# Encoder block on 8 cores: the meta keys' V products split into two 64-row halves and moved beside the K products

## The chip, the cores and the metric

One Trainium2 chip, 8 cores, one launch of one program. Each core works on its own part of the batch (one whole prompt sequence of 2048 tokens and one half of a sample sequence of 8192) and no core waits for another. The metric is the device time of the slowest core in microseconds (us), the median of several runs. Engines are named as the profile names them: PE (TensorE; PEld is its weight load), DVE (VectorE), ACT (ScalarE), POOL (GpSimd) and SP (SyncE, here only a DMA queue).

## The reference

One layer, run on both request groups with shared weights: RMSNorm, one input projection, a pooling mixer and a neighbourhood attention side by side, gates, an output projection with a residual, and a last RMSNorm. The change is in the attention alone:

```
# q, k, v: (B, L, H, 64), L = 16 meta tokens + T; real tokens form a (ROWS, 64) grid
def row_block(r):
    rs = clip(r - 4, 0, rows - 8)                 # 8 grid rows of keys
    s_grid = einsum('bqhd,bkqjhd->bhqkj', q_r, k_r) * scale + bias     # 8 x 16 keys each
    s_meta = einsum('bqhd,bmhd->bhqm', q_r, km) * scale + mbias        # 16 meta keys
    p = softmax(concatenate([s_meta, s_grid], -1))
    return einsum('bhqm,bmhd->bqhd', p[..., :16], vm) + einsum('bhqkj,bkqjhd->bqhd', p_grid, v_r)
```

So every query takes part in 128 grid keys and 16 meta keys. The output of a query is the sum of a V product over the grid keys and one over the meta keys, divided by the sum of all the exponentials.

## The kernel before, in words

The program has three stages. Stage one normalises the tokens, makes K and V and stores them. Stage two makes Q and the pooled projection z and does the attention. Stage three does the gates and the output projection. All instructions are recorded in program order, each goes into the queue of its engine, and every engine works its queue off in that order. A helper (`Sched`) derives the waits from the names each operation reads and writes: a read waits for the last write of the same name in the recorded order.

In stage two the queries are cut into 14 tiles of query rows (`TILES`, counted from 0). Tiles 0 and 4 use one chunk of keys ("one-chunk tiles"), the other twelve use two. In tiles 0, 4, 5 and 13 a unit has 64 queries, in the others 128. A tile has 8 units: 4 column groups `s` by 2 head groups `G` of 8 heads. There are 112 units, numbered `ui`. The keys of a unit come in blocks of 128 (`unit_blocks`): 2 blocks in a one-chunk tile; in a two-chunk tile 3 for `s` 0 and 3 and 4 for `s` 1 and 2. The third block of `s` 0 and 3 takes 64 keys of each of two chunks ("the combined block"); in the unit with `G` = 1 it is put first. A block of a unit is a step, and there are 368 steps.

A step `(ui, b)` does the following. `p2_qk` forms the K products of 8 heads on PE: two heads at a time, one on array rows 0 to 63 and one on 64 to 127, because a head is 64 long (the trace writes 64*128; those of a combined block have 64 output rows and are written 64*64). ACT takes the exponential of the 8 heads out of two PSUM banks into `PT[ui % 2]`, slice `b`, and DVE multiplies it in place by the exponentials of the bias (`FT`, `CT` or `XT`). Then come "fills": matmuls of 128x512 of the Q and z projections (L904, L927), some 3 to 9 a step, until the tile's list is used up. Last come V products of the unit before: `p2_pv` multiplies a block's `PT` slice with V, one head at a time (65 columns; column 65 gives the sum of the exponentials), and adds them up in banks 4 and 5.

The steps are recorded in groups of two: K products of both steps, then fills and V products of the first, then of the second. So within a group of steps `(ui, 2)` and `(ui + 1, 0)` the K products, exponentials and multiplies of both stand ahead of all V products of the group.

The meta keys' exponentials of a tile lie in `PM`, 16 keys of 8 heads on 128 partitions (32 to a pair of heads). `VMb` holds the meta keys' V on the same partitions, zero outside a head's own 65 columns, so that one matmul over 128 rows and 260 columns gives the meta part of four heads. `p2_pvmeta` is that matmul. It opens each bank's sum. Bank 4 takes the four even heads (`par` = 0), bank 5 the four odd ones. `p2_norm` takes the reciprocal of the sums out of a bank (L1052) and multiplies (L1054) into `ATT`.

`pv_steps` says which V products of unit `ui - 1` go into step 0, 1 and 2 of unit `ui`: in step 0 the meta product of bank 4 and all blocks but the last, in step 1 the last block, the norm of bank 4, the meta product of bank 5 and two blocks, in step 2 the rest and the norm of bank 5. In a unit of two blocks everything of step 2 goes into step 1.

The finished `ATT` is stored from the queue of SP, in tiles 9 to 12 from the queue of POOL.

## Time and profile before

| | us |
|---|---|
| median of 3 runs | 1763.38 (1757.53 to 1893.18) |
| the profiled execution, device time | 1761.12 |
| its span on the slowest core, first to last instruction | 1759.6 |
| spans of all cores | 1748.7 to 1759.6 |
| PE busy | 1690.0 (96%) |
| stage two, 438 to 1058 us of the span: PE busy | 590.5 of 620.0 |

The profiled execution is 1.5 us longer than its span, for what lies ahead of the first and behind the last instruction, and 2.3 us under the median. The granted TensorE clock is 0.986 of full over the whole span of this core. In the rows "busy" is the time in which at least one instruction of a group ran. A matmul's own length (some 190 to 380 ns) is longer than the distance to the next one that starts behind it, because they run in a pipeline: what a matmul costs PE is read from one start to the next.

### The profile page before, as it was taken

How to read it: one execution, taken by the hardware profiler on the slowest of the kernel's cores; microseconds unless marked ns; L12 is line 12 of the kernel's file. 1: busy time of each engine (PE TensorE's matmuls, PEld its weight loads, DVE VectorE, ACT ScalarE, POOL GpSimd, SP SyncE). 2: the span in 40 equal slices, each digit the busy share in tenths (PEclk: the TensorE clock that was granted, in tenths of full speed). 3: DMA queues.
4: the chain of work that ended last, by engine and by line, in shares of the span. 5: the costliest groups of instructions: out<-in, count | busy, mean ns of one | idle time of the engine just before them, and what ended most of it. 6: DMA issues, size and time to landing. Idle time of an engine off the chain costs nothing.

```text
span 1759.6 us, 39346 instructions; the slowest of 8 cores (1748.7 to 1759.6 us)
## 1 busy us (share of the span) xinstructions
PE 1690.0 (96%) x13906; PEld 873.7 (50%) x13906; DVE 1000.9 (57%) x1907; ACT 821.3 (47%) x1219; POOL 124.3 (7%) x202
## 2 busy tenths in 40 slices
PE   7799999999999899999999998999999999999998
PEld 3344544444455555655666554444444444444443
DVE  3354544442466665766777755556655566556654
ACT  3256666331256765777777762332333233323332
POOL 1011021111100000000000020000000000000000
PEclk9899999999999999999999999999999999999999
DMA  9689778663555566666543479733454346524521
GB/s 264 218 239 282 226 240 238 200 169 136 172 141 157 149 166 176 154 179 176 146 123 98 132 214 266 187 114 109 126 174 148 86 128 162 168 88 129 139 96 61
DMA packets 163814, 289.21 MB, mean 164 GB/s; under 512 B 70627, under 2 KB 92643, under 8 KB 155047
## 3 DMA queue, kind: packets, MB, share of 16 engines
q1 hardware_dynamic: 110167, 155.04, 31.2%
q0 software_dynamic: 37184, 95.66, 19.1%
q10 hardware_dynamic: 16272, 35.99, 6.6%
q8 instruction: 116, 1.90, 0.5%
q14 instruction: 75, 0.61, 0.1%
HBM read 194.90 MB, written 100.90 MB: 168 GB/s over the span
## 4 chain that ended last, share of the span: by engine, by line
PE 79%; issue 5%; ACT 5%; DVE 4%; DMA 4%; SPq 2%; ACTq 1%; DVEq 0%; POOL 0%; POOLq 0%
PE bankpair L433 19%; PE bankpair L927 9%; PE bankpair L588 9%; PE bankpair L620 9%; PE bankpair L407 9%; PE bankpair L380 9%; PE bankpair L904 5%; PE bankpair L1039 3%; PE bankpair L1008 3%; ACT sb_PT L1014 2%; DMA sb_XSG<-xt 2%; DVE sb_PT L1020 1%; PE bankpair L567 1%; PE bankpair L368 1%; DVE sb_QT L217 1%
## 5 line engine op out<-in xcount | busy, mean ns | idle before, releaser
L1014 ACT ACTIVATE sb_PT<-bankpair 128x1024 bf16<-128x1024 f32 (+1 forms) x368 | 318.8, 921 | 152.8 <-PE bankpair L1008 112.1
L433 PE MATMUL bankpair<-sb_Wo,sb_MIX 128*128 128x512 bf16 x1536 | 336.9, 381 | 3.7 <-DVE sb_MIX L417 3.7
L433 PEld LDWEIGHTS bankpair<-sb_Wo,sb_MIX 128*128 128x128 bf16 x1536 | 150.8, 98 | 187.8 <-issue 9.1
L1020 DVE TENSOR_TENSOR sb_PT<-sb_PT,sb_FT 128x1024 bf16<-128x1024 bf16 (+1 forms) x264 | 174.8, 666 | 106.1 <-ACT sb_PT L1014 103.3
L927 PE MATMUL bankpair<-sb_Wz,sb_HT 128*128 128x512 bf16 x768 | 199.6, 388 | 3.0 <-ACT sb_PM L957 2.7
L588 PE MATMUL bankpair<-sb_HT,sb_Wk 128*128 128x512 bf16 (+1 forms) x832 | 189.7, 383 | 9.5 <-ACT sb_Wk L219 5.0
L904 PE MATMUL bankpair<-sb_HT,sb_Wq 128*128 128x512 bf16 x768 | 194.7, 382 | 1.7 <-DVE sb_QT L217 1.7
L620 PE MATMUL bankpair<-sb_Wv,sb_HT 128*128 128x512 bf16 x816 | 184.0, 379 | 0.0
L380 PE MATMUL bankpair<-sb_HT,sb_Wg 128*128 128x512 bf16 x768 | 182.6, 381 | 0.0
L441 ACT ACTIVATE sb_junk<-sb_Y 128x1024 bf16<-128x1024 f32 x48 | 50.7, 1057 | 266.3 <-DVE sb_Y L436 266.3
L407 PE MATMUL bankpair<-sb_HT,sb_Wg 128*128 128x512 bf16 x768 | 167.7, 379 | 0.0
L1039 PEld LDWEIGHTS bankpair<-sb_VP,sb_PT 128*128 128x128 bf16 x2496 | 122.2, 98 | 51.1 <-issue 4.1
L1039 PE MATMUL bankpair<-sb_VP,sb_PT 128*128 128x65 bf16 x2496 | 135.6, 194 | 3.1 <-issue 3.1
L588 PEld LDWEIGHTS bankpair<-sb_HT,sb_Wk 128*128 128x128 bf16 x832 | 80.9, 100 | 100.2 <-issue 18.6
L436 DVE TENSOR_TENSOR sb_Y<-bankpair,sb_XR 128x512 f32<-128x512 f32 x96 | 66.1, 689 | 112.2 <-PE bankpair L433 112.2
L620 PEld LDWEIGHTS bankpair<-sb_Wv,sb_HT 128*128 128x128 bf16 x816 | 79.7, 98 | 95.0
L1008 PE MATMUL bankpair<-sb_QT,sb_KR 64*128 64x128 bf16 (+3 forms) x3328 | 111.8, 213 | 13.8 <-ACT sb_PT L1014 13.5
L407 PEld LDWEIGHTS bankpair<-sb_HT,sb_Wg 128*128 128x128 bf16 x768 | 74.3, 98 | 87.8
L411 ACT ACTIVATE sb_TH<-bankpair 128x512 f32<-128x512 f32 x96 | 57.3, 597 | 114.5 <-PE bankpair L407 92.7
L1054 DVE TENSOR_TENSOR sb_ATT<-bankpair,sb_rec 128x256 bf16<-128x256 f32 (+1 forms) x224 | 94.7, 423 | 27.8 <-DVE sb_rec L1052 10.3
L380 PEld LDWEIGHTS bankpair<-sb_HT,sb_Wg 128*128 128x128 bf16 x768 | 69.6, 98 | 71.4 <-issue 1.5
L386 ACT ACTIVATE sb_TH<-bankpair 128x512 f32<-128x512 f32 x96 | 56.1, 596 | 100.9 <-PE bankpair L380 69.4
(104 smaller groups left out, 1736.3 us busy)
## 6 DMA issues: line engine op xcount, KB each, us to landing
sb_X<-xall SPq DMA_DIRECT2D x51, 512.0 KB, 5.7
sb_XR<-xall SPq DMA_DIRECT2D x48, 512.0 KB, 3.6
y<-sb_O POOLq DMA_DIRECT2D x48, 512.0 KB, 3.2
sb_HT<-hT_s SPq DMA_DIRECT2D x23, 1024.0 KB, 6.1
sb_KR<-kT_s SPq DMA_DIRECT2D x14, 1024.0 KB, 7.2
sb_UW<-u_s SPq DMA_DIRECT2D x54, 256.0 KB, 7.8
kT_s<-sb_KTs POOLq DMA_DIRECT2D x13, 1024.0 KB, 5.1
v_s<-sb_Vs POOLq DMA_DIRECT2D x49, 260.0 KB, 3.5
```

Of the source, the lines that this page charges most:

```text
L380: S.op('tensor', lambda e, pg=pg, dc=dc, kc=kc, cs=cs, N=N: e.matmul(banks[pg][:, 0:N], Wg[dc // 2][:, kc, dc % 2 * 128:dc % 2 * 128 + 128 ...
L407: S.op('tensor', lambda e, pg=pg, fc=fc, kc=kc, cs=cs, N=N: e.matmul(banks[pg][:, 0:N], Wg[4 + fc // 2][:, kc, fc % 2 * 128:fc % 2 * 128 + ...
L433: S.op('tensor', lambda e, po=po, kc=kc, cg=cg, j=j: e.matmul(banks[po][:, :], MIX[:, kc, j * 128:(j + 1) * 128], Wo[kc // 4][:, kc % 4, c ...
L588: S.op('tensor', lambda e, pb=pb, fc=fc, kc=kc, hs=hs, N=N: e.matmul(banks[pb][:, 0:N], Wk[:, kc, fc * 128:(fc + 1) * 128], HT[hs][:, kc, ...
L620: S.op('tensor', lambda e, pb=pb, cg=cg, kc=kc, hs=hs, j=j: e.matmul(banks[pb][:, :], HT[hs][:, kc, j * 128:(j + 1) * 128], Wv[:, kc, cg * ...
L904: S.op('tensor', lambda e: e.matmul(banks[pb][:, :], Wq[:, kc, fc * 128:(fc + 1) * 128], HT2[ci % 2][:, kc, :], start=(kc == 0), stop=(kc ...
L927: S.op('tensor', lambda e: e.matmul(banks[pb][:, :], src[:, kc, p * 128:(p + 1) * 128], Wz[:, kc, cg * 512:(cg + 1) * 512], start=(kc == 0 ...
L1008: S.op('tensor', lambda e, jj=jj, fc=fc, i=i, cell=cell, ncell=ncell, p0=p0, par=par: e.matmul(banks[2 * sp + par][p0:p0 + 64 * ncell, jj ...
L1014: S.op('scalar', lambda e: e.activation(out=PT[ps][0:nk, bi, :, 0:n].rearrange('p (a b) q -> p a b q', a=2), in_=bank2[sp][0:nk, :].rearra ...
L1020: S.op('vector', lambda e: e.tensor_tensor(out=PT[ps][0:nk, bi, :, 0:n], in0=PT[ps][0:nk, bi, :, 0:n], in1=bl['E'](hs), op=ALU.mult), read ...
L1039: S.op('tensor', lambda e, jj=jj, h=h: e.matmul(banks[4 + par][:, jj * 65:(jj + 1) * 65], PT[ps][0:nk, bi, par * 4 + jj, :], bl['V'][0:nk, ...
L1054: S.op('vector', lambda e: e.tensor_tensor(out=ATT[at][0:n, :].rearrange('p (a b c) -> p a b c', a=8, b=2)[:, 4 * G:4 * G + 4, par, :], in ...
```

## The change

The meta products are split by rows instead of by bank. Bank 4 now takes heads 0 to 3 of the group and bank 5 heads 4 to 7. The meta rows of heads 0 to 3 lie on partitions 0 to 63 and those of heads 4 to 7 on 64 to 127, so each bank's meta product needs 64 rows only, and the two stand together, on the two halves of the array. `VMb` shrinks from 1040 to 528 columns. The V products of the blocks are as many as before, in another order of heads, and are shared out by a new function `pv_plan`:

- unit `ui - 1`, when unit `ui` has 2 blocks (15 units, those ahead of a unit of tile 0 or 4): the meta products stand behind the K products of the group of steps 0 and 1, open both banks, and all V products and norms go into steps 0 and 1;
- when `ui` has 3 or 4 blocks and its first step is the first of a group (72 units): the meta products stand at the head of the group with step 2, ahead of its K products, and close bank 4, whose norm is recorded directly behind them. All V products of bank 5 go into step 2;
- when its first step is the second of a group (24 units): the meta products stand behind the K products of the group with step 1, and the rest is as before;
- the last unit has its V products behind the loop, as before.

In one-chunk tiles the combined block's V products now take all 128 rows; the lower 64 rows of `VC` are set to zero on DVE for that (4 times). All stores of `ATT` go through the queue of SP.

```
@@ v_combo
+                    if len(tl['ch']) == 1:
+                        S.op('vector', lambda e: e.memset(VC[w][64:128, :], 0.0), writes=[('VC', w, 1)])
@@ p2_pvmeta, p2_pv
-                def p2_pvmeta(ui, par):
-                    S.op('tensor', lambda e: e.matmul(
-                        banks[4 + par][:, 0:260], PM[t % 2][:, G, s, :], VMb[:, G, par, :, :].rearrange('p a b -> p (a b)'),
-                        start=True, stop=False), reads=[('PM', t % 2, G)] + VMR, writes=[PS(4 + par)])
+                def p2_pvmeta(ui, opens, ends=False):
+                    for half in range(2):
+                        rows = slice(64 * half, 64 * half + 64)
+                        S.op('tensor', lambda e, half=half, rows=rows: e.matmul(
+                            banks[4 + half][:, 0:260], PM[t % 2][rows, G, s, :], VMb[rows, G, 0:260],
+                            start=(opens or half == 1), stop=(ends and half == 0)), reads=[('PM', t % 2, G)] + VMR, writes=[PS(4 + half)])
-                def p2_pv(ui, par, bi, last):
+                def p2_pv(ui, half, bi, opens, last):
-                    for jj in range(4):
+                    for q in range(4):
+                        jj, par = 2 * half + q // 2, q % 2
@@ pv_steps is replaced by
+                def pv_plan(ui):
+                    nb = nblk[ui]
+                    nn = nblk[ui + 1] if ui + 1 < len(units) else 2
+                    even = ui + 1 == len(units) or first_step[ui + 1] % 2 == 0
+                    opens = even and nn == 2
+                    lead = [lambda bi=bi: p2_pv(ui, 0, bi, bi == 0 and not opens, False) for bi in range(nb - 1)]
+                    tail = lambda last: [lambda: p2_pv(ui, 0, nb - 1, False, last)]
+                    half1 = [lambda bi=bi: p2_pv(ui, 1, bi, False, bi == nb - 1) for bi in range(nb)]
+                    n0, n1 = [lambda: p2_norm(ui, 0)], [lambda: p2_norm(ui, 1)]
+                    if nn == 2:
+                        return 0 if even else 1, opens, {0: lead, 1: tail(True) + n0 + half1 + n1}
+                    if even:
+                        return 2, False, {0: lead, 1: tail(False), 2: half1 + n1}
+                    return 1, False, {0: lead, 1: tail(True) + n0 + half1[:2], 2: half1[2:] + n1}
@@ the loop over groups of two steps
                     for ui, b in steps[k:k + 2]:
                         if b == 0:
                             unit_begin(ui)
+                        if b == 2 and ui > 0 and pv_plan(ui - 1)[0] == 2:
+                            p2_pvmeta(ui - 1, False, True)
+                            p2_norm(ui - 1, 0)
+                    for ui, b in steps[k:k + 2]:
                         p2_qk(ui, b)
+                    for ui, b in steps[k:k + 2]:
+                        if b < 2 and ui > 0 and pv_plan(ui - 1)[0] == b:
+                            p2_pvmeta(ui - 1, pv_plan(ui - 1)[1])
                     for ui, b in steps[k:k + 2]:
                         unit_step(ui, b)
```

In the listings below `sb_VMb` with 128x260 is a meta product, `sb_KR` a K product, `sb_VP` or `sb_VC` with 128x65 a V product of a block, and `sb_Wz` or `sb_Wq` a fill.

On PE, in tile 0, around the K products of a group of a one-chunk tile. Before:

```order
L1039 MATMUL bankpair<-sb_VC,sb_PT 128x65 x4
L1027 MATMUL bankpair<-sb_VMb,sb_PM 128x260 [waits s_vector]
L1039 MATMUL bankpair<-sb_VP_0,sb_PT 128x65 x4
L1039 MATMUL bankpair<-sb_VC,sb_PT 128x65 x4
L1008 MATMUL bankpair<-sb_QT,sb_KR 128x64 x16
L927 MATMUL bankpair<-sb_Wz,sb_HT_0 128x512 [waits s_scalar]
L927 MATMUL bankpair<-sb_Wz,sb_HT_0 128x512 x7
L904 MATMUL bankpair<-sb_HT_1,sb_Wq 128x512 [waits d__HT2_1_False_,s_scalar]
L1027 MATMUL bankpair<-sb_VMb,sb_PM 128x260 [waits s_vector]
```

The same place after:

```order
L1042 MATMUL bankpair<-sb_VC,sb_PT 128x65 x4
L1042 MATMUL bankpair<-sb_VP_0,sb_PT 128x65 x4
L1042 MATMUL bankpair<-sb_VC,sb_PT 128x65 x4
L1011 MATMUL bankpair<-sb_QT,sb_KR 128x64 x16
L1031 MATMUL bankpair<-sb_VMb,sb_PM 128x260 [waits s_vector] x2
L930 MATMUL bankpair<-sb_Wz,sb_HT_0 128x512 [waits s_scalar]
L930 MATMUL bankpair<-sb_Wz,sb_HT_0 128x512 x7
L907 MATMUL bankpair<-sb_HT_1,sb_Wq 128x512 [waits d__HT2_1_False_,s_scalar]
```

Before, a bank's meta product stands behind fills; after, both stand directly behind the K products, and both wait for DVE, which reads the banks for the norms of the unit before.

On PE, at the entry of tile 1, the group of steps `(8, 2)` and `(9, 0)`, two combined blocks, seen from the K products on. Before:

```order
L1008 MATMUL bankpair<-sb_QT,sb_KR 64x128 [waits s_scalar]
L1008 MATMUL bankpair<-sb_QT,sb_KR 64x128 x15
L927 MATMUL bankpair<-sb_Wz,sb_HT_1 128x512 x6
L927 MATMUL bankpair<-sb_Wz,sb_HT_1 128x512 [waits s_scalar]
L927 MATMUL bankpair<-sb_Wz,sb_HT_1 128x512 x3
L1027 MATMUL bankpair<-sb_VMb,sb_PM 128x260 [waits s_vector]
L1039 MATMUL bankpair<-sb_VP_0,sb_PT 128x65 x4
```

The same place after, with the meta products ahead of it:

```order
L1042 MATMUL bankpair<-sb_VC,sb_PT 128x65 x4
L1031 MATMUL bankpair<-sb_VMb,sb_PM 128x260
L1031 MATMUL bankpair<-sb_VMb,sb_PM 128x260 [waits s_vector]
L1011 MATMUL bankpair<-sb_QT,sb_KR 64x128 [waits s_scalar]
L1011 MATMUL bankpair<-sb_QT,sb_KR 64x128 x15
L930 MATMUL bankpair<-sb_Wz,sb_HT_1 128x512 x5
L1042 MATMUL bankpair<-sb_VP_2,sb_PT 128x65 [waits s_vector]
L1042 MATMUL bankpair<-sb_VP_2,sb_PT 128x65 x3
L1042 MATMUL bankpair<-sb_VC,sb_PT 128x65 x4
L930 MATMUL bankpair<-sb_Wz,sb_HT_1 128x512
```

Between the two steps' fills there now stand V products of unit 7 (bank 5, all its blocks), and the first of them waits for DVE. They read `PT[1]`, slice 0, and the exponential and the multiply of step `(9, 0)`, recorded ahead of them in the same group, write that slice. The same happens wherever a unit of 3 blocks starts on the first step of a group: two units in each of the twelve two-chunk tiles.

## Rows read from the trace of the kernel before

**Rows 1.** The page: PE's busy time, share of the span, instructions.

```profile
PE 1690.0 (96%) x13906; PEld 873.7 (50%) x13906; DVE 1000.9 (57%) x1907; ACT 821.3 (47%) x1219; POOL 124.3 (7%) x202
```

**Rows 2.** Stage two by windows: length, busy PE, PEld, DVE, ACT, POOL, clock, DMA.

```profile
438.00:1058.00 620.00, 590.54 (x8154) 350.96 (x8152) 410.67 (x1010) 406.18 (x531) 39.94 (x50) 0.99 0.57 156
```

**Rows 3.** The group of meta products: busy us, mean ns, idle before.

```profile
L1027 PE MATMUL bankpair<-sb_VMb,sb_PM 128*128 128x260 bf16 x224 | 61.7, 275 | 7.1 <-DVE sb_rec L1052 4.4 <-DVE sb_ATT L1054 2.4
```

**Rows 4.** Timeline, tile 7, group of two combined blocks: start us, length us, engine.

```profile
754.53 0.64 PE L1008 MATMUL bankpair<-sb_QT,sb_KR 64*64 64x128 bf16 x32
755.10 1.25 PE L927 MATMUL bankpair<-sb_Wz,sb_HT 128*128 128x512 bf16 x5
756.19 0.29 PE L1039 MATMUL bankpair<-sb_VP,sb_PT 128*128 128x65 bf16 x4
756.31 1.24 PE L927 MATMUL bankpair<-sb_Wz,sb_HT 128*128 128x512 bf16 x5
...
757.15 0.69 DVE L1020 TENSOR_TENSOR sb_PT<-sb_PT,sb_CT 128x1024 bf16<-128x1024 bf16 x1 [0.22 <-ACT sb_PT L1014]
757.39 0.27 PE L1027 MATMUL bankpair<-sb_VMb,sb_PM 128*128 128x260 bf16 x1
757.50 0.41 PE L1039 MATMUL bankpair<-sb_VP,sb_PT 128*128 128x65 bf16 x8
...
757.84 0.62 PE L1008 MATMUL bankpair<-sb_QT,sb_KR 64*128 64x128 bf16 x16
```

**Rows 5.** Timeline, tile 5 (64 queries), the same kind of group.

```profile
703.18 1.04 PE L904 MATMUL bankpair<-sb_HT,sb_Wq 128*128 128x512 bf16 x4
...
703.99 0.91 DVE L1020 TENSOR_TENSOR sb_PT<-sb_PT,sb_XT 128x512 bf16<-128x512 bf16 x2
704.05 0.41 PE L1039 MATMUL bankpair<-sb_VP,sb_PT 128*128 128x65 bf16 x8
```

**Rows 6.** Timeline, tile 4 (one chunk), K products, first fill, norm of bank 5.

```profile
640.12 0.53 PE L1008 MATMUL bankpair<-sb_QT,sb_KR 64*128 64x64 bf16 x16
...
640.59 1.25 PE L904 MATMUL bankpair<-sb_HT,sb_Wq 128*128 128x512 bf16 x5
640.83 0.42 DVE L1054 TENSOR_TENSOR sb_ATT<-bankpair,sb_rec 128x256 bf16<-128x256 f32 x1
...
657.00 1.04 PE L904 MATMUL bankpair<-sb_HT,sb_Wq 128*128 128x512 bf16 x4
...
658.67 0.42 DVE L1054 TENSOR_TENSOR sb_ATT<-bankpair,sb_rec 64x256 bf16<-64x256 f32 x1
```

**Rows 7.** Timeline of PE, tile 4: V products on 64 rows; K products of whole blocks.

```profile
641.91 1.24 PE L904 MATMUL bankpair<-sb_HT,sb_Wq 128*128 128x512 bf16 x5
643.08 0.29 PE L1039 MATMUL bankpair<-sb_VC,sb_PT 64*128 64x65 bf16 x4
643.31 0.28 PE L1027 MATMUL bankpair<-sb_VMb,sb_PM 128*128 128x260 bf16 x1
...
650.61 0.41 PE L1008 MATMUL bankpair<-sb_QT,sb_KR 64*128 64x64 bf16 x16
650.95 1.04 PE L904 MATMUL bankpair<-sb_HT,sb_Wq 128*128 128x512 bf16 x4
```

**Rows 8.** What PE waited for: us in total, times, longest us.

```profile
PE bankpair L1027 <- DVE sb_rec L1052: 4.4, 5, 2.1
```

**Rows 9.** Timeline of PE: four waits, each in square brackets.

```profile
633.72 0.22 PE L1039 MATMUL bankpair<-sb_VP,sb_PT 128*128 128x65 bf16 x2 [1.39 <-issue]
...
772.68 0.40 PE L1008 MATMUL bankpair<-sb_QT,sb_KR 64*128 64x128 bf16 x8 [1.85 <-ACT sb_PT L1014]
773.60 0.54 PE L1008 MATMUL bankpair<-sb_QT,sb_KR 64*128 64x128 bf16 x8 [0.52 <-ACT sb_PT L1014]
...
1042.51 0.37 PE L1039 MATMUL bankpair<-sb_VP,sb_PT 128*128 128x65 bf16 x7 [1.68 <-issue]
```

**Rows 10.** Windows around two of them; the clock is third from the end.

```profile
773.72:777.13 3.41, 3.41 (x23) 1.56 (x20) 3.13 (x9) 1.56 (x2) 0.00 (x0) 0.50 1.02 321
...
1040.00:1045.00 5.00, 3.32 (x51) 1.91 (x48) 1.73 (x6) 2.40 (x5) 0.16 (x1) 1.00 1.03 368
```

More of the change, by code:

```diff
@@ L241, in build_program @@
         second += [('VP0_%d' % q, [128, VW], BF16) for q in range(3)] + [('VC%d' % w, [128, VW], BF16) for w in range(2)]
-        second += [('VMb', [128, 2, 2, 4, 65], BF16), ('KM', [128, KC, 32], BF16), ('HTm', [128, KC, 128], BF16)]
+        second += [('VMb', [128, 2, 264], BF16), ('KM', [128, KC, 32], BF16), ('HTm', [128, KC, 128], BF16)]
         second += [('PM%d' % i, [128, 2, 4, 128], BF16) for i in range(2)]
@@ L872, in build_program @@
                         S.op('sync', lambda e, jj=jj, par=par, p0=p0: e.dma_start(
-                            out=VMb[p0:p0 + 16, :, par, jj, :],
+                            out=VMb[p0:p0 + 16, :, (2 * (jj % 2) + par) * 65:(2 * (jj % 2) + par) * 65 + 65],
                             in_=v_d[VM + 16:VM + 32, :].rearrange('m (g q f) -> m g q f', g=2, q=8)[:, :, 2 * jj + par, :]),
@@ L985, in unit_blocks @@
                         b = dict(nk=nk, parts=[(i, 7 * w, 1, 64 * k) for k, i in enumerate(tl['ch'])], V=VC[w],
[L986 removed]
+                                 vres=[('VC', w, k) for k in range(2)])
                         if tl['xs'] is None:
@@ L1048, in p2_norm @@
                     at = (ui // 2) % 2
-                    ab = 4 + par
+                    ab = 4 + half
                     accv = lambda: banks[ab][0:n, 0:260].rearrange('p (a b) -> p a b', a=4)
-                    rs = slice(par * 4, par * 4 + 4)
+                    rs = slice(half * 4, half * 4 + 4)
+                    c0 = (8 * G + 4 * half) * 64
                     S.op('vector', lambda e: e.reciprocal(rec[0:n, rs], accv()[:, :, 64]),
-                         reads=[PS(ab)], writes=[('rec', par)])
+                         reads=[PS(ab)], writes=[('rec', half)])
@@ L1054, in p2_norm @@
                     S.op('vector', lambda e: e.tensor_tensor(
-                        out=ATT[at][0:n, :].rearrange('p (a b c) -> p a b c', a=8, b=2)[:, 4 * G:4 * G + 4, par, :], in0=accv()[:, :, 0:64],
+                        out=ATT[at][0:n, c0:c0 + 256].rearrange('p (a c) -> p a c', a=4), in0=accv()[:, :, 0:64],
                         in1=rec[0:n, rs].unsqueeze(2).to_broadcast([n, 4, 64]), op=ALU.mult),
-                         reads=[PS(ab), ('rec', par)], writes=[('ATT', at)])
-                    if G == 1 and par == 1:
+                         reads=[PS(ab), ('rec', half)], writes=[('ATT', at)])
@@ L1059, in p2_norm @@
+                    if G == 1 and half == 1:
                         t0 = tl['t0']
[L1060 removed]
+                        late.append(lambda: S.op('sync', lambda e: e.dma_start(
                             out=at_d[t0:t0 + n * 4, :].rearrange('(r c) f -> r c f', c=64)[:, 16 * s:16 * s + 16, :], in_=ATT[at][0:n, :]),
                              reads=[('ATT', at)], writes=[('at_d', t, s)], dma=('sA', at)))
[L1064 to L1076 removed]
@@ new lines, in build_program @@
+                nblk = [len(unit_blocks(u)) for u in units]
+                first_step = [sum(nblk[:i]) for i in range(len(units))]
+                def pv_plan(ui):
[12 more added lines that the diff above has]
+                    return 1, False, {0: lead, 1: tail(True) + n0 + half1[:2], 2: half1[2:] + n1}
@@ L1109, in unit_step @@
                             late.pop(0)()
-                    for f in pv_steps(ui - 1)[b] if ui > 0 and b < 3 else []:
+                    for f in pv_plan(ui - 1)[2].get(b, []) if ui > 0 else []:
                         f()
-                    if nb == 2 and b == 1 and ui > 0:
-                        for f in pv_steps(ui - 1)[2]:
-                            f()
                     if b == nb - 1:
```

31 lines of the change are left out of this document (7 added, 24 removed).

## The prediction, made before the changed kernel ran

> **What bounds the kernel now.** The page comes first: PE is busy 96% of the span, no other engine over 57% [rows 1]. All edits lie in stage two, so the windows come next: there PE is busy 590.5 of 620.0 us, DVE 411 and ACT 406 [rows 2]. PE works its queue off in order. So whatever PE saves or loses in stage two moves the end by as much, unless it falls into the 30 us in which PE waits there already. The change has to be read as PE time saved, and as PE waits removed and added. The timeline shows what things cost PE, from one start to the next: a meta product 0.11 us (757.39 to 757.50), a V product 0.03 us (four of them from 756.19 to the next fill at 756.31), a fill 0.22 us (five from 755.10 to 756.19) [rows 4].
>
> **Meta products on two halves of the array.** Before there are 224 [rows 3], 24.6 us at 0.11. After there are 112 pairs. K products already run in such pairs: the 32 quarter-array ones of [rows 4] take 0.57 us up to the first fill, 0.02 each, where 128 columns alone take more than a V product of 65 columns (0.03). So I take a pair for the price of one and save 0.11 each. In the 14 pairs that wait between their two halves (below) nothing is saved: 98 x 0.11 = **-10.8**. The bounds are -12.3 and, if the halves run one after the other, 0.
>
> **Switches of the array.** After eight V products at 0.03 (0.24) the K products start 0.34 behind the first (757.50 to 757.84), so going from whole rows to half rows costs 0.10 [rows 4]. The V products on 64 rows show both ways: they start 0.09 late behind five fills (641.91 + 1.08 = 642.99, start 643.08), and take 0.23 instead of 0.12 up to the next meta product [rows 7]. The change makes the 64-row V products of the one-chunk tiles whole. Half of them (8 places) stood between whole-row work: 8 x 0.20 = **-1.6**; the other half stood next to K products and only moves the switch. A change of the output width costs as well: the 16 K products of two whole blocks take 0.34 (650.61 to 650.95) [rows 7], the 16 of a whole and a combined block 0.47 (640.12 to 640.59) [rows 6]. A meta product is 64 rows by 128, a combined block's K product 64 by 64. They now stand side by side in 24 groups of the two-chunk tiles and 7 of the one-chunk tiles: 31 x 0.10 = **+3.1**. Elsewhere the meta pair shares the half-row stretch of its K products and adds no switch. Against this change the Trainium skill says (TensorEngine Tiling (Array Packing), "Key Properties") that changing the tiling mode drains the array, and it lists 64x128 and 64x64 as modes of their own. It gives no time. By the rule alone the moved pairs at combined blocks would pay a drain each, as I have it; the trace agrees, with 0.13 for such a change.
>
> **Waits that go.** Meta products find PE idle for 7.1 us, of which 4.4 and 2.4 end with the reciprocal and the multiply of a norm on DVE [rows 3]. The longest single wait, 2.1 [rows 8], is the last unit's, which has no cover after the change either. The other 4.7 lie where the tile's fills are used up, behind K products or between V products, and the meta products leave those places: **-4.7**, with the new waits of the one-chunk tiles counted in full below.
>
> **A new wait behind the K products in one-chunk tiles.** There both banks are opened directly behind the K products, with no fill between. Bank 5 must first be free of the norm of the unit before, which is recorded at the end of the group before. In the row that fits best the first fill starts at 640.59 and that norm's multiply ends at 640.83 + 0.42 = 641.25 [rows 6]. PE would come to the pair some 0.2 earlier than the fill did (no switch back yet, no meta product between the V products), so it waits 0.66 + 0.2 = 0.9. In the second row DVE is late (657.00 against 659.09): 2.3. The new wait itself lets DVE catch up, so I stay near the first and take 1.0. It happens in 14 units (6 in tile 0, 8 in tile 4): **+14**, bounds 9 and 20. Queued behind it on PE are the fills, and behind those the next K products. Neither ACT nor DVE profits.
>
> **A new wait in 24 groups of the two-chunk tiles.** This is the largest term. The plan for "3 or 4 blocks" puts all V products of bank 5 of unit `ui - 1` into step 2 of `ui`. When `ui` has 3 blocks, that group's second step is `(ui + 1, 0)`, and it writes the same `PT` slice 0 that the first of these V products reads. The listing shows that V product waiting for DVE behind five fills. Before, the V products of slice 0 were in step 1, a group earlier. So PE now waits for two exponentials and two multiplies of the same group. In [rows 4] the fills start at 755.10; the V products after them started at 756.19; the second multiply ends at 757.15 + 0.69 = 757.84. With 0.06 for the signal PE waits until 757.90: 1.71 us behind five fills, 1.93 behind four, 2.14 behind three. Working the list of fills out step by step gives 8 groups of 128 queries with five, 9 with four, 3 with three: 13.7 + 17.4 + 6.4 = 37.5. For 64 queries [rows 5] gives 704.90 + 0.06 against 704.05, 0.91 behind four, 0.7 behind five, 1.1 behind three: one, one and two groups, 3.8. Together **+41.3**. Nothing covers it: behind the waiting product on PE stand the other V products and five fills that are ready. The bounds are 36, if the exponentials start 0.2 earlier, and 43.
>
> That ready work doesn't pass shows in [rows 9]: at 633.72 a V product waits 1.39 us for something no engine row shows (a load of V, I suppose) with K products queued behind it. The Trainium skill has the same as a rule (TensorE: Matmul & The Clock Gate, "Step-by-step: what each phase is for"): only weight loads are pulled ahead, matmuls stay in program order. If matmuls could pass, the term would be 0.
>
> One wait is taken over: 633.72 lies behind the K products of such a group in tile 3, and the new wait of over 2 us ends later: **-1.4**.
>
> **The clock.** Behind waits of 1.85 and 0.52 us close together (772.68, 773.60) the granted clock is 0.50 for 3.41 us, the 1.2 GHz level [rows 9, 10]. Behind single waits of 1.39 and 1.68 it stays at 1.00, 2.4 GHz [rows 9, 10]. A stretch at half clock costs at most 1.7 us of matmul time; I take 1.5. The 20 new waits of 1.7 to 2.1 lie between these cases. I let five of them cost a stretch: **+7.5**, bounds 0 and 30.
>
> **At nothing.** The norms change only their columns. DVE gets four memsets of 64 rows and is busy 66% of the stage [rows 2]. `VMb` is half as long. The 16 stores that move from POOL's queue to SP's wait there for a norm, as 40 others do in tiles 0 to 8 and 13, and only loads for later tiles stand behind them; should one of these come late, it costs a wait like that at 1042.51, 1.7 us [rows 9]. Spreading the V products evenly over two groups gives PE 0.25 us more work in the lighter group of tiles 3 and 13, where PE waits for exponentials; some 1 us, not counted.
>
> **The sum.** -10.8 - 1.6 + 3.1 - 4.7 + 14 + 41.3 - 1.4 + 7.5 = +47.4. On the profiled execution's 1761.1 this gives **1808**, 2.5% over the median of 1763.4, to which the profiled execution stands 2.3 lower. A measurement of this kernel can tell about 2% from no change, that is 1799 on the slow side.
>
> **Rivals.**
> First, the clock never falls: the sum without 7.5 is 1801. For it speak the 1.39 and 1.68 that left the clock at 1.00. 25%.
> Second, the clock falls behind nearly every new wait, as behind 772.68: 20 x 1.5 in place of 7.5 gives 1831. 13%.
> Third, it does not get slower: the V products of bank 5 find slice 0 already multiplied when PE comes to them, and the 24 waits aren't there. That needs some 13 fills (2.8 us) between K products and V products, or a multiply done within 1.1 us of the K products; [rows 4] shows five fills and 2.7 us. It also holds if I misread which operation the wait is for. Then 41.3, 1.4 and 7.5 fall away and the sum is 0: 1761, and 1754 if the one-chunk waits are half as long. 8%.
> Fourth, the change does not do what it says: the two halves run one after the other and the pairs cost 0.22. Then 10.8 is lost: 1819. Against it stand the K products of [rows 4]. 4%.
> The forecast itself, 1808, has 46%; the rest, 4%, is for late loads and what I don't see.
>
> **Range and chances.** The lower bounds of the costs (36, 9, clock 0, -12.3) give +27, that is 1788; the upper ones (43, 20, clock 30) give +80, 1841. With the third rival left out, and a little of the second, 1788 to 1835 should hold 8 in 10. Slower by over 2%, above 1799: the forecast, the second and fourth rival and over half of the first, 75%. Within 2%: the third rival, the lower part of the first and of the forecast, 23%. Faster by over 2% would need 35 us saved, more than all savings together: 2%.
>
> **What the profile of the changed kernel would show.** The group of V products should have waits for DVE's multiply of `PT`, 24 of them, 40 us in all, 1.7 to 2.1 us each at 128 queries. The meta products should wait for the norm's multiply 14 times behind K products in tiles 0 and 4, some 1 us each. The pair's second half should start within 0.02 us of the first and the next matmul 0.11 to 0.2 behind it. Stage two should be 667 us long and the other two stages unchanged. The clock row should show some five more stretches at 0.50. It would be wrong if PE's waits for DVE in stage two stay under 20 us; or if the time gained between them is larger than 20 us; or if the clock falls so often that it outweighs the waits.

## The result and the profile after

The changed kernel takes 1818.7 us in the median of 4 runs (1817.0 to 1822.1), the kernel before 1763.0 beside it. The ratio is 1.033, interval 1.032 to 1.035. The forecast was 1808, the range 1788 to 1835. The profiled execution took 1817.6, its slowest core is core 3 with a span of 1816.1 us. Ratios are formed from executions alone in which no half of the chip had a lower granted clock than the other, so a median beside them can contain slower ones.

The changed kernel doesn't compute all of the attention: in 24 of the 112 units the V products of four heads take 128 keys with exponentials that belong to another unit (shown below). Its slowdown is therefore in large part the price of a fault.

The page's PE row, which answers to [rows 1]:

```profile
PE 1695.8 (93%) x13906; PEld 866.3 (48%) x13906; DVE 1008.6 (56%) x1911; ACT 821.7 (45%) x1219; POOL 114.6 (6%) x186
```

PE has nearly the same work (1690.0 before) in a longer span. POOL has 16 instructions less, the stores. Stage two by windows, which answers to [rows 2] (length, then busy PE, PEld, DVE, ACT, POOL, then clock):

```profile
438.00:1114.00 676.00, 593.87 (x8139) 342.20 (x8137) 416.85 (x1008) 406.34 (x532) 28.13 (x30) 0.98 0.52 144
```

Length minus busy PE was 29.5 us before and is 82.1 now. So nearly all of the loss is waiting. I counted stage two on every core, from its first matmul with `Wq` to the first of line 380: 617.5 us before and 676.8 now, in the mean of the eight cores. This mean is used below as the length of stage two. What lies ahead of it is unchanged (436.5 and 436.6 us). What lies behind it is 3.3 us shorter (700.2 and 696.9), of which 2.0 is less idle time of PE (4.3 and 2.3); so the whole lost a little less than stage two.

PE's waits over the whole span, the view of [rows 8] (waiting line, releaser: us in all, times, longest). L1042 is the V products, L1031 the meta products, L1011 the K products:

```profile
PE bankpair L1042 <- DVE sb_PT L1023: 39.5, 25, 2.1
PE bankpair L1011 <- ACT sb_PT L1017: 18.1, 26, 2.3
...
PE bankpair L1031 <- DVE sb_rec L1056: 10.9, 15, 2.4
...
PE bankpair L1031 <- DVE sb_ATT L1058: 5.2, 15, 0.4
PE bankpair L1042 <- DVE sb_ATT L1058: 2.8, 1, 2.8
```

The first row didn't exist before. It is the forecast's largest term, with 24 of its 25 waits. The third and fourth row are the one-chunk waits (14 units and the last one, each half once). The last row was not forecast.

**The wait for slice 0.** The timeline of a group of tile 7 in which the next unit's first block is a combined block (start us, length us, engine, line, idle before in square brackets):

```profile
787.00 0.28 PE L1031 MATMUL bankpair<-sb_VMb,sb_PM 64*128 64x260 bf16 x2
...
787.22 0.64 PE L1011 MATMUL bankpair<-sb_QT,sb_KR 64*64 64x128 bf16 x32
...
787.79 1.25 PE L930 MATMUL bankpair<-sb_Wz,sb_HT 128*128 128x512 bf16 x5
787.80 1.02 ACT L1017 ACTIVATE sb_PT<-bankpair 128x1024 bf16<-128x1024 f32 x1 [0.56 <-PE bankpair L1011]
...
788.72 1.02 ACT L1017 ACTIVATE sb_PT<-bankpair 128x1024 bf16<-128x1024 f32 x1
788.93 0.69 DVE L1023 TENSOR_TENSOR sb_PT<-sb_PT,sb_CT 128x1024 bf16<-128x1024 bf16 x1 [0.82 <-ACT sb_PT L1017]
789.84 0.69 DVE L1023 TENSOR_TENSOR sb_PT<-sb_PT,sb_CT 128x1024 bf16<-128x1024 bf16 x1 [0.22 <-ACT sb_PT L1017]
...
790.68 0.29 PE L1042 MATMUL bankpair<-sb_VC,sb_PT 128*128 128x65 bf16 x4 [1.63 <-DVE sb_PT L1023]
```

The five fills would let the V product start at 787.79 + 5 x 0.216 = 788.87. It starts at 790.68, 0.15 behind the end of the second multiply (790.53). That is 1.81 us from one start to the next, and the bracket says 1.63: the idle column counts from the modelled end of the last fill, some 0.17 later than the next matmul could have started. Worked out from the starts, the 24 waits of core 3 cost 43.2 us, and so they do on the other cores (43.1 to 43.2).

The wait is also the sign of the fault. The helper lets a read wait for the last write in recorded order, and here that write is the later unit's. So in these 24 units the products of slice 0 of four heads (bank 5) take the exponentials of unit `ui + 1` in place of their own, those of `ui - 1`, which are overwritten by then. The sums of exponentials for those heads come from the same products and are wrong with them. The wait that the helper derived keeps the read behind the write; it doesn't make it the right write.

**The one-chunk tiles.** The timeline in tile 4, with what DVE does meanwhile:

```profile
678.52 0.55 PE L1042 MATMUL bankpair<-sb_VP,sb_PT 128*128 128x65 bf16 x12
678.79 0.76 DVE L217 CAST sb_QT<-bankpair 128x256 bf16<-128x256 f32 x2 [1.81 <-PE bankpair L907]
679.00 0.41 PE L1011 MATMUL bankpair<-sb_QT,sb_KR 64*128 64x64 bf16 x16
...
679.46 0.17 DVE L1056 RECIPROCAL sb_rec<-bankpair 64x4 f32<-64x4 f32 x1
679.73 0.42 DVE L1058 TENSOR_TENSOR sb_ATT<-bankpair,sb_rec 64x256 bf16<-64x256 f32 x1
680.07 0.17 DVE L1056 RECIPROCAL sb_rec<-bankpair 64x4 f32<-64x4 f32 x1
...
680.29 0.27 PE L1031 MATMUL bankpair<-sb_VMb,sb_PM 64*128 64x260 bf16 x1 [0.88 <-DVE sb_rec L1056]
680.34 0.42 DVE L1058 TENSOR_TENSOR sb_ATT<-bankpair,sb_rec 64x256 bf16<-64x256 f32 x1
...
680.91 0.27 PE L1031 MATMUL bankpair<-sb_VMb,sb_PM 64*128 64x260 bf16 x1 [0.34 <-DVE sb_ATT L1058]
...
681.11 1.04 PE L907 MATMUL bankpair<-sb_HT,sb_Wq 128*128 128x512 bf16 x4
```

Both halves wait, one for the norm of bank 4, the other for that of bank 5, and the fills stand behind them. The second half starts 0.15 behind the end of bank 5's multiply (680.34 + 0.42 = 680.76). The first starts 0.14 behind the end of bank 4's multiply (679.73 + 0.42 = 680.15); the row names the reciprocal of bank 5 because that one ended last before it. What PE loses is set by bank 5's multiply, the last of the chain. From the last K product to the first matmul behind the pair, less the 0.26 that this takes without a wait, the 14 units lose 19.0 us in the mean of the cores. On core 3 eight of them lose 1.0 to 1.3 and six 1.5 to 2.0. In five of the six DVE is at casts of Q when the norms could begin, as at 678.79 here; in the sixth it is at a multiply of `PT`.

**The pair.** Where it doesn't wait (tile 7):

```profile
769.63 0.29 PE L1042 MATMUL bankpair<-sb_VP,sb_PT 128*128 128x65 bf16 x4
769.85 0.28 PE L1031 MATMUL bankpair<-sb_VMb,sb_PM 64*128 64x260 bf16 x2
769.97 0.61 PE L1011 MATMUL bankpair<-sb_QT,sb_KR 64*128 64x128 bf16 x16
```

Two meta products take 0.12 up to the next matmul (0.003 + 0.118), one took 0.11 before; their starts lie 3 ns apart. The four V products ahead take 0.22 instead of 0.12 [rows 4]: the switch to half rows, paid here and not behind the pair. From a pair to the K products of a combined block (787.00 to 787.22) it is 0.21 instead of 0.12: the change of shape.

**A store on SP.** The timeline of tile 12 (SPq is SP's queue):

```profile
1036.94 0.42 DVE L1058 TENSOR_TENSOR sb_ATT<-bankpair,sb_rec 128x256 bf16<-128x256 f32 x1
...
1039.26 10.76 SPq L790 DMA_DIRECT2D sb_HT<-hT_s  x4
...
1050.12 0.83 SPq L1064 DMA_DIRECT2D at_s<-sb_ATT  x1
...
1052.64 0.64 SPq L1064 DMA_DIRECT2D at_s<-sb_ATT  x1
...
1056.55 0.42 DVE L1058 TENSOR_TENSOR sb_ATT<-bankpair,sb_rec 128x256 bf16<-128x256 f32 x1 [6.39 <-DMA at_s<-sb_ATT]
...
1057.12 0.41 PE L1042 MATMUL bankpair<-sb_VP,sb_PT 128*128 128x65 bf16 x8 [2.85 <-DVE sb_ATT L1058]
```

There are two `ATT` buffers. The one that the norm at 1056.55 writes was filled by 1037.36, and its store was issued at 1050.12: four loads of `HT` stood ahead of it in SP's queue, and their issuing took 10.8 us (the store at 1052.64 is of the other buffer). DVE's norm waits until the store has landed, and PE waits for the norm. DVE waits so on all eight cores, by 3.1 to 6.7 us. PE waits behind it on six: 2.3 to 3.1 us on four, 0.4 and 0.7 on two.

### The profile page after: what moved, and what is told of

Same layout as the page of the kernel before. It is cut to its first block, busy times and chain, and to the rows that moved or that the text cites. A ratio compares the mean times of both kernels' runs of the same rounds, so it can differ in the third digit from the quotient of the medians.

```text
span 1816.1 us, 39324 instructions; the slowest of 8 cores (1805.1 to 1816.1 us)
## 1 busy us (share of the span) xinstructions
PE 1695.8 (93%) x13906; PEld 866.3 (48%) x13906; DVE 1008.6 (56%) x1911; ACT 821.7 (45%) x1219; POOL 114.6 (6%) x186
## 4 chain that ended last, share of the span: by engine, by line
PE 78%; ACT 5%; issue 5%; DMA 4%; DVE 4%; SPq 3%; ACTq 1%; DVEq 0%; POOL 0%; POOLq 0%
PE bankpair L433 18%; PE bankpair L407 8%; PE bankpair L380 8%; PE bankpair L620 8%; PE bankpair L588 8%; PE bankpair L907 7%; PE bankpair L930 7%; PE bankpair L1042 5%; PE bankpair L1011 3%; ACT sb_PT L1017 3%; SPq L479 1%; DVE sb_PT L1023 1%; DMA sb_WS<-w_in 1%; PE bankpair L368 1%; DMA at_s<-sb_ATT 1%
## 5 line engine op out<-in xcount | busy, mean ns | idle before, releaser
L907 PE MATMUL bankpair<-sb_HT,sb_Wq 128*128 128x512 bf16 x768 | 199.1, 389 | 2.6 <-DVE sb_QT L217 2.5
L930 PE MATMUL bankpair<-sb_Wz,sb_HT 128*128 128x512 bf16 x768 | 195.8, 381 | 3.0 <-ACT sb_PM L960 2.7
L1042 PE MATMUL bankpair<-sb_VP,sb_PT 128*128 128x65 bf16 x2496 | 129.4, 195 | 25.9 <-DVE sb_PT L1023 23.0
L1042 PEld LDWEIGHTS bankpair<-sb_VP,sb_PT 128*128 128x128 bf16 x2496 | 114.0, 99 | 81.2 <-issue 34.3
L1011 PE MATMUL bankpair<-sb_QT,sb_KR 64*128 64x128 bf16 (+3 forms) x3328 | 112.1, 213 | 18.6 <-ACT sb_PT L1017 18.1
L411 ACT ACTIVATE sb_TH<-bankpair 128x512 f32<-128x512 f32 x96 | 57.3, 597 | 112.2 <-PE bankpair L407 91.5
L1011 PEld LDWEIGHTS bankpair<-sb_QT,sb_KR 64*128 64x128 bf16 (+1 forms) x3328 | 82.9, 98 | 52.4 <-issue 44.9
```

The source lines that it names most:

```text
L907: S.op('tensor', lambda e: e.matmul(banks[pb][:, :], Wq[:, kc, fc * 128:(fc + 1) * 128], HT2[ci % 2][:, kc, :], start=(kc == 0), stop=(kc ...
L930: S.op('tensor', lambda e: e.matmul(banks[pb][:, :], src[:, kc, p * 128:(p + 1) * 128], Wz[:, kc, cg * 512:(cg + 1) * 512], start=(kc == 0 ...
L1011: S.op('tensor', lambda e, jj=jj, fc=fc, i=i, cell=cell, ncell=ncell, p0=p0, par=par: e.matmul(banks[2 * sp + par][p0:p0 + 64 * ncell, jj ...
L1042: S.op('tensor', lambda e, q=q, jj=jj, par=par, h=h: e.matmul(banks[4 + half][:, q * 65:(q + 1) * 65], PT[ps][:, bi, par * 4 + jj, :], bl[ ...
```

## The experiments

Line numbers move by a few between kernels: V products are L1039 (before and e7; L1041 in e6), L1042, L1043 or L1044, meta products L1027 (L1029 in e6), L1031, L1032 or L1033. Differences in us between two kernels are differences of their ratios to the kernel before, times 1761.

| kernel | ratio to before, interval | stage two, us |
|---|---|---|
| before | 1 | 617.5 |
| after | 1.0331, 1.0316 to 1.0345 | 676.8 |
| e7, before with the late slice 0 | 1.0213, 1.0188 to 1.0238 | 656.2 |
| e1, after with slice 0 in time | 1.0134, 1.0107 to 1.0161 | 639.7 |
| e2, e1 with the pair behind fills | 1.0054, 1.0040 to 1.0069 | 627.2 |
| e4, e1 with the stores on POOL | 1.0116, 1.0085 to 1.0146 | 634.1 |
| e5, e1 with another order of heads | 1.0113, 1.0094 to 1.0133 | 637.5 |
| e6, before with whole combined blocks | 1.0021, 0.9994 to 1.0048 | 613.8 |
| e9, after with full-row meta products | 1.0351, 1.0323 to 1.0379 | 678.3 |
| e3b, pair closes both banks | 1.0007, 0.9995 to 1.0019 | 619.7 |
| e10, e3b with e4 and e5 | 0.9984, 0.9957 to 1.0010 | 614.2 |

### The late slice 0 alone (e7)

```
-                        steps[1 if bi < 2 else 2].append(lambda bi=bi: p2_pv(ui, 1, bi, bi == nb - 1))
+                        steps[1 if bi < 2 and not late5 else 2].append(lambda bi=bi: p2_pv(ui, 1, bi, bi == nb - 1))
```

`late5` holds where the next unit has three blocks and starts a group. Like the change, this kernel lets slice 0 of four heads be read too late in 24 units.

> The kernel before with one part of the change alone: in those 24 groups the V products of bank 5 all go into step 2. So in 24 units the V products of slice 0 of four heads take the exponentials that the later unit has put there, as in the changed kernel. Theory A: 24 waits of 1.7 to 2.2 us, +43 us, 1763 becomes 1806. Theory B: PE finds other cover or the products are ready, under +20 us, below 1783.

Measured: 1799.7 us, +37.5. PE's waits in its trace:

```profile
PE bankpair L1039 <- DVE sb_PT L1020: 39.4, 24, 2.1
```

The same 24 waits, with no pair and no new order of heads in the kernel, make two thirds of the whole loss (37.5 of 58.3).

### Slice 0 in time (e1)

```
+                    if even and nn == 3:
+                        h1 = [lambda bi=bi: p2_pv(ui, 1, bi, bi == 0, bi == nb - 1) for bi in range(nb)]
...
+                        return 2, False, {0: lead, 1: tail(False) + h1[:2], 2: h1[2:] + n1}
```

> The changed kernel with one part undone: where the unit after it has three blocks and starts a group, the V products of bank 5 for the first two blocks go back into step 1, so the slice 0 that the next unit but one writes is read a group earlier; its first V product opens bank 5 and the meta product adds to it. All else stays as changed. Theory A (the 24 waits of the first such V product for the multiply are the loss): start to start they add 43 us in the trace after, so 1818.7 falls to about 1775, and the waits of the V products for the multiply are gone. Theory B (the loss lies in the half-row pairs, the array switches and the closer one-chunk order, the wait is only where it shows): less than 20 us come back, 1800 or more, and PE waits elsewhere in its place.

Measured: 1786.5 us, 35 less than the changed kernel (37 in stage two), not 43. Its waits (core 3):

```profile
PE bankpair L1032 <- DVE sb_ATT L1059: 12.1, 29, 0.9
PE bankpair L1011 <- ACT sb_PT L1017: 11.1, 17, 1.6
PE bankpair L1032 <- DVE sb_rec L1057: 10.4, 14, 2.1
...
PE bankpair L1043 <- DVE sb_ATT L1059: 4.2, 1, 4.2
```

The V products' waits for `PT` are gone. The meta products' wait for the norm's multiply, however, went from 5.2 us in 15 to 12.1 in 29. In groups that a unit starts at the second step, the pair opens bank 5 directly behind the K products, and its second half needs the norm of the unit before. In e1 it waits for that norm's multiply in most of these groups, by 0.05 to 0.9 us. In the changed kernel the multiply has ended 0.26 to 2.1 us earlier in all of them, because the long wait shortly before let DVE catch up. So 7 us of the 43 come back as another wait.

### The pair behind the fills of its group (e2)

```
-                        if b < 2 and ui > 0 and pv_plan(ui - 1)[0] == b:
+                        if b == 1 and ui > 0 and pv_plan(ui - 1)[0] == b:
...
+                    if b == 0 and ui > 0 and pv_plan(ui - 1)[0] == 0:
+                        p2_pvmeta(ui - 1, True)
```

> The first of these kernels, and in the one-chunk tiles the pair of meta products stands behind the fills of step 0 instead of directly behind the K products. Theory A: the 14 waits for the norms go. By the trace after they cost some 20 us from start to start (idle 13.5), and two switches of 0.1 each come back in 15 units, +3: 17 us under the first kernel, about 1758. Rival: the norms are late for another reason (casts of Q on DVE), and the wait moves behind the fills: under 5 us gained.

Measured: 14 us less than e1 (12.4 in stage two). Core 3:

```profile
PE bankpair L1032 <- DVE sb_ATT L1059: 9.4, 21, 0.9
...
PE bankpair L1032 <- DVE sb_rec L1057: 3.7, 3, 2.1
```

The waits for the reciprocal fall from 14 to 3, those for the multiply by 8. The fills between K products and pair cover the norm, as they did before the change. This confirms what the one-chunk waits are. Of the 19 us that the starts give, 14 come back: in the last unit that is affected in either tile no fills are left, so it waits as before (some 3 us for both), and each moved pair pays two more switches of 0.09.

### The stores back on POOL (e4)

```
-                        late.append(lambda: S.op('sync', lambda e: e.dma_start(
+                        late.append(lambda: S.op('gpsimd' if 9 <= t < 13 else 'sync', lambda e: e.dma_start(
```

> The first of these kernels, with the stores of tiles 9 to 12 back in the queue of POOL. In the trace after one norm of tile 12 waits 6.4 us for a store of the same buffer and PE 2.9 us for that norm. If the moved stores cause this, the slowest core gains 2 to 4 us over the first kernel and that wait is gone; if not, the two are equal within 1 us and the wait stays.

Measured: 3 us less than e1 (5.6 in stage two, of which part is noise). The wait of the V products for the norm (4.2 us on core 3 of e1, 4.1 in the mean of the cores) is gone from the trace on all of them, and so is DVE's wait for the store. The intervals of e1 and e4 overlap, so the time alone doesn't decide it; the row does.

### The order of heads (e5)

```
-                    for q in range(4):
+                    for q in (0, 2, 1, 3):
```

> The kernel of e1_slice0_in_time with the four V products of a block and bank issued in the order of columns 0, 2, 1, 3, so that their weights are slices 0, 1, 4, 5 of the block in turn, in place of 0, 4, 1, 5. In the profile of the changed kernel the V products of one group of four start 33 ns apart against 31 before. Theory A: the jump between slices from one weight load to the next costs the 2 ns; then the mean falls back to 31 ns and the time by 4 to 5 us against e1. Theory B: it is something else (the heads of one bank, or what stands around the groups): no difference over 2 us.

Measured: 3.7 us less than e1, with intervals that overlap, so the spacing in the trace has to decide. Busy PE of the V products alone, windows of core 3, first e1, then e5:

```profile
438.00:1120.00 682.00, 147.47 (x2944) 0.98 0.58 160
```

```profile
438.00:1120.00 682.00, 143.14 (x2944) 0.98 0.58 161
```

The mean distance of two V products that stand next to each other (2,490 to 2,620 places on each core) is 31.2 ns before, 32.9 in the changed kernel, 32.6 in e1 and 31.2 in e5. Without the stretches at half clock it is 30.9, 32.1, 32.1 and 30.6. So the order in which the four heads are issued costs 1.3 to 1.5 ns for each V product, some 4 us in all. Theory A's number holds, its reason isn't shown. In groups of four that run without a gap at full clock, the first step takes 29.4 ns and the second 34 in every one of these kernels. The difference lies in the third step (32.5 in e1, 29.2 in e5) and in the one to the next group (32.7 and 29.4). Theory A's jump by four slices, 0 to 4, is the first step of a group in e1, and costs nothing there. The edit changes at once the order of the weight slices, of the columns of V and of the columns in the bank. The bank's columns are written in turn in the slow kernels as in the kernel before, so their order is not the cause by itself; between the other two nothing here decides.

### Whole combined blocks alone (e6)

```
+                        S.op('vector', lambda e: e.memset(VC[w][64:128, :], 0.0), writes=[('VC', w, 1)])
...
-                            banks[4 + par][:, jj * 65:(jj + 1) * 65], PT[ps][0:nk, bi, par * 4 + jj, :],
+                            banks[4 + par][:, jj * 65:(jj + 1) * 65], PT[ps][:, bi, par * 4 + jj, :],
```

> The kernel before with one part of the change alone: in the one-chunk tiles the lower half of the combined V block is zeroed and the V products of combined blocks run over 128 rows instead of 64. The prediction gives this -1.6 us (eight places, two switches of the array of 0.10 each). Theory: 1761.5, within the noise of no difference; the row of V products at 641.91 to 643.08 loses its 0.09. Rival: the 128-row products read rows of PT that another unit wrote and so take on waits; then the time rises and V products show waits for DVE.

Measured: 1762.5 us, no difference that can be told, and no new wait in the trace. The size comes from the trace of before: 8 times a V product is followed 126 ns later by one on 64 rows, and 8 times one on 64 rows 121 ns later by a meta product, where 29 are usual: 16 x 0.09 = 1.5 us.

### Full-row meta products in the new places (e9)

```
-                            banks[4 + half][:, 0:260], PM[t % 2][rows, G, s, :], VMb[rows, G, 0:260],
+                            banks[4 + half][:, 0:260], PM[t % 2][:, G, s, :], VMb[:, G, half, 0:260],
```

> The changed kernel with the pairing alone undone: the two meta products of a unit stand where the change puts them, but each runs over all 128 rows (the rows of the other four heads are zero in VMb). If a pair costs what one product did, the second product adds 0.11 in 98 of 112 pairs, 10.8 us, and the two switches between half rows and whole rows are no more than before: 1818 + 9 to 12, about 1828. If the pair had not run side by side (the fourth rival of the prediction) there is no difference: 1818.

Measured: 1823.3 us, 3.5 us over the changed kernel with intervals that overlap, and not 9 to 12. Part of the difference is an oversight in the expectation: without the half-row pair the changes of shape (24 x 0.09) go as well, and a pair saves 0.099 and not 0.11, so 7.5 was to be expected. PE's timeline of this kernel on its core 2:

```profile
746.02 0.40 PE L1031 MATMUL bankpair<-sb_VMb,sb_PM 128*128 128x260 bf16 x2
746.25 1.24 PE L930 MATMUL bankpair<-sb_Wz,sb_HT 128*128 128x512 bf16 x5
```

Two full-row products take 0.23 up to the next fill. In the pairs that don't wait the second product starts 0.110 behind the first, against 0.003, and the starts around the meta products add up to 7 us more than in the changed kernel once the waits are left out. The kernel was also at half clock for less of stage two (21.8 us per core against 28.2), which is worth up to 3 us the other way. The time alone doesn't decide about the pair; the starts do.

### The pair closes both banks (e3b)

```
+                        if b == 0 and ui > 1 and pv_plan(ui - 2)[0] == 3:
+                            p2_pvmeta(ui - 2, False, True)
+                            p2_norm(ui - 2, 0)
+                            p2_norm(ui - 2, 1)
                    for ui, b in steps[k:k + 2]:
                        p2_qk(ui, b)
```

> Made from the kernel of e1_slice0_in_time. The pair of meta products no longer opens a bank behind the K products: except before a one-chunk unit that starts within a group it stands at the head of the group that follows the unit's V products, ahead of the K products, and closes bank 4 or both; the norms of what it closes stand directly behind it, so that K products and fills lie between a norm and the next product that needs its bank. If what is left of the loss in e1 (stage two 640 us against 617) is norm waits, some 20 us start to start in the one-chunk tiles and 8 to 10 in the odd groups, this gives them back: about 1760 (1752 to 1770), the meta products' waits for DVE under 4 us and stage two near 613. Rival: the norms stand now ahead of the multiplies of their group on DVE and delay them; then V products and K products wait for PT in their place, and the time stays near 1780.

Measured: 1762.7 us, 22 less than e1 and the same as before (stage two 619.7, not 613). Core 3:

```profile
PE bankpair L1011 <- ACT sb_PT L1017: 12.8, 20, 1.8
PE bankpair L1044 <- DVE sb_ATT L1060: 8.0, 11, 4.0
PE bankpair L1044 <- DVE sb_rec L1058: 4.8, 6, 2.2
```

No meta product waits any more. The V products that open a bank behind it still do: 12.8 us with the 4.0 of the store, where the meta products before waited 6.8 (4.4 and 2.4 in [rows 3]). The rival, multiplies delayed by the norms, is not in the trace: no V product waits for `PT`, and the K products' wait for exponentials is 13.8 in the mean of the cores against 13.7 before. The 4.0 is the store on SP's queue again.

### All together (e10)

The diff is that of e4 and e5 on top of e3b.

> The kernel of e3b_pair_closes_both_banks with the two small things that stood alone so far: the stores of tiles 9 to 12 back in POOL's queue (3.2 us in e4_stores_back_on_pool), and the heads of a bank issued in the order 0, 2, 1, 3 (3.7 us in e5_heads_order_before). If the three add up it is 7 us below e3b, about 1753, under the kernel before by some 8 us: what the change was after, pairs at 0.11 instead of 0.22 and no wait for a norm, once nothing is given back. Rival: the waits that e3b leaves hide the V products' gain, and it stays within 2 us of e3b.

Measured: ratio 0.9984, 4 us under e3b (5.5 in stage two) and 3 under the kernel before, whose interval reaches from 8 us faster to 2 us slower. The intervals of e3b and e10 overlap; that the two small edits help here as well is likely by stage two, and by about half of the 7 us expected. By the starts the pairs save 9.7 and spend 2.2 on changes of shape, and the banks' waits take a few more. It is not shown to be faster than before.

## Why the prediction was right, term by term

The forecast was on the right side, for the reason given, and 11 us low (1808 against 1818.7; in stage two +47.4 against +59.3). Its own terms add up to +28.1 and +77.6 at the bounds, where it has +27 and +80; the measured time is far from both.

| term | forecast | measured | from |
|---|---|---|---|
| meta products in pairs | -10.8 | -9.7 | 98 x (2 x 0.110 before, 0.121 after), starts |
| V products on 64 rows | -1.6 | -1.5 | starts of before; e6 can't tell it |
| changes of shape | +3.1 | +2.2 | 24 x 0.093; the seven in one-chunk tiles lie in a wait |
| old norm waits | -4.7 | -4.7 | the forecast's row; none in the old places |
| one-chunk waits | +14 | +19 | starts of after; e2: -14 |
| late slice 0 | +41.3 | +43.2 | starts of after; e7: +37.5; e1: -35 |
| load wait absorbed | -1.4 | -1.3 | V products' waits with no engine as releaser, mean of the cores: 2.1 before, 0.8 after |
| clock | +7.5 | +6.6 | an estimate: 28.2 us at half clock per core against 13.2, at 1.5 for 3.41 |
| order of heads | none | +3.7 | 2,944 x 1.25 ns, at full clock; e5: -3.7 |
| stores on SP | 0 | +1.5 | waits for the norm, mean of the cores (four at 2.3 to 3.1); e4: -3 |

The measured column adds up to +59.0, against 59.3 from the lengths of stage two. So close an agreement is in part luck: the K products' waits for exponentials grew by 1.6 us (13.7 to 15.3 in the mean of the cores) and those of `Wq` matmuls for `QT` by 1.0, and neither is in the table.

**Late slice 0.** The step was right in kind, number (24) and size. The prediction names the write that the product waits for, but not what follows from it, that the exponentials read are the wrong unit's. e7 shows it alone. The third rival, that the waits aren't there, is refuted by its 39.4 us. That PE's matmuls wait in program order with ready fills behind them shows at 787.79 to 790.68 in the timeline; the Trainium skill says the same (TensorE: Matmul & The Clock Gate, "Step-by-step: what each phase is for"), and the trace agrees with its 1.81 us.

**One-chunk waits.** This is the term that was mis-sized most, by 5 us. The step that failed is "so I stay near the first and take 1.0": it took nearly the lowest value for every unit. Eight units are like that row (1.0 to 1.3); in six DVE comes to the norms later, mostly behind casts of Q, and they cost 1.5 to 2.0. That a wait stands at each half doesn't add to it, since both end with the same chain of norms.

**"At nothing".** Two things stood there, or weren't seen, that cost. The stores moved to SP's queue were said to cost only if a load came late. What came late was the store itself, which stood behind loads in that queue, and the next norm into the same buffer waits for it. The sum also had no term for the new order of heads within a bank: the working looked at how many V products there are and over how many rows, not at the order in which heads follow one another. Together +5 us, as much as the one-chunk waits lacked.

**Clock.** The second rival (a stretch at half clock behind nearly every wait) is refuted: in units of 3.41 us there are 8.3 stretches per core, 4.4 more than before, where it needed 20. The first (none) is too. Windows of core 3, the clock third from the end, the first around the wait at 790.68, the second behind one of 1.85 us:

```profile
788.00:795.00 7.00, 5.37 (x67) 3.07 (x66) 2.79 (x6) 4.28 (x6) 0.00 (x0) 1.00 0.48 146
550.46:553.88 3.42, 3.42 (x40) 2.17 (x36) 1.36 (x4) 0.17 (x1) 0.00 (x0) 0.50 0.14 14
```

Of 192 waits for slice 0 on the eight cores, some 25 were followed by such a stretch within 1.4 us. What tells these from the others I can't say.

**Switches and pairs.** The fourth rival, halves one after the other, is refuted by the starts 3 ns apart, where the full-row products of e9 lie 0.110 apart. The Trainium skill says that a change of the tiling mode drains the array (TensorEngine Tiling (Array Packing), "Key Properties"). The trace agrees in that such a change costs time: 0.09 us between 64x128 and 64x64, as between whole and half rows. At 24 places this is nearly a quarter of what the pairs save.

What stays open: why the V products' spacing depends on the order of heads, when the clock falls, and the 3 us by which e10 stays short of the sum of its parts.

## What to carry to other kernels

When the order of accumulating products is changed so that they run in one piece, ask of each buffer slice that they read who writes it next and in which group: a product moved one group later met the next unit's writer, and 24 such places cost over four times what the whole idea saves. Worse, it read that writer's values: a wait derived from recorded order guards the order and not the meaning, so a new wait for a writer of another unit is a fault to mend before it is a cost to count. With slice 0 read in time (e1) the same idea costs 1.3% and not 3.3%. A product that opens a bank wants other work of its engine (fills) between the norm that frees the bank and itself; one that closes it doesn't, but the next one that opens the bank does (e3b). A store moved to another queue also takes on what stands ahead of it there. Removing one wait shows those that it hid, here 7 of 43 us, so take a wait's worth from a run without it, not from its row.

## What the runs showed of the hardware that was not expected

- V products of 65 columns with weights from slices 0, 4, 1, 5 of a tile start 32.1 ns apart in the mean at full clock, and 30.6 with 0, 1, 4, 5 (e1 and e5), some 4 us over 2,944 of them. Only the third step of a group of four and the one to the next group differ (32.5 and 32.7 against 29.2 and 29.4), and the columns of V change their order with the slices, so which of the two does it is open.
- Two products on opposite halves of the rows start 3 ns apart and take 0.121 us together up to the next product of the same shape, against 0.110 for one product over all rows.
- Going from 64x128 to 64x64 costs 0.093 us, as much as going from whole to half rows (0.09 to 0.1 behind V products and fills).
- The idle time in brackets before a matmul is 0.16 to 0.18 us short of what the wait costs from start to start, when a fill stands ahead (1.63 against 1.81).
- Four loads of `HT` took 10.8 us to issue in SP's queue (1039.26 to 1050.02); a store of 128 rows behind them kept its buffer from 1037.36 to 1056.55. With the stores of tiles 9 to 12 in POOL's queue (e4) no norm waited for a store on any core.
